# A two-layer block on one Trainium2 core: a new order in the even mixer, from the last input block to the output projection

## The reference, cut to what matters

```
def even_mixer(hn, w_in, w_conv, g_v, w_s, b_s, w_out):
    z = hn @ w_in
    b_gate, c_gate, x_in, u, v = split(z)                 # five blocks of 512 columns
    y_a = b_gate * causal_conv3(c_gate * x_in, w_conv)    # "conv half"
    u = gelu(u); v = rmsnorm_per_head(gelu(v), g_v)
    mixed = einsum('hts,nshd->nthd', tril(w_s), v) + b_s  # per head, chunks of 128 positions
    y_b = u * mixed                                       # "spatial half"
    return concatenate([y_a, y_b]) @ w_out
```

## Time and profile before

| | us |
|---|---|
| median of 3 runs | 1367.24 (1366.95 to 1367.79) |
| the profiled execution: span from its first to its last instruction | 1366.5 |
| TensorE busy | 1263.6 (92%) |
| VectorE busy | 752.9 (55%) |
| ScalarE busy | 489.6 (36%) |
| output projection of the even mixer, first product to the transposes behind it | 95.26 to 118.63 |

### The profile page before, as it was taken

How to read it: one execution, slowest core, us unless ns; L and a number is a source line. 1 busy time by engine, 2 the same in 40 slices (tenths; PEclk the granted TensorE clock), 3 DMA queues, 4 the chain that set the end, 5 groups by cost and what they waited for, 6 DMA issues and landing times.

```text
span 1366.5 us, 16254 instructions
## 1 busy us (share of the span) xinstructions
PE 1263.6 (92%) x6228; PEld 879.6 (64%) x6228; DVE 752.9 (55%) x1442; ACT 489.6 (36%) x835; POOL 27.0 (2%) x60
## 2 busy tenths in 40 slices
PE   5978999999898899999987997779999999999995
PEld 4967888876676777888866985644444444445442
DVE  4765877786657667777866998532122212222222
ACT  4424444444446444444445753411111111111111
POOL 0000000000000000000001200000000000000000
PEclk9989999999998699999998999899999999999998
DMA  8447767652431247777533311879999999999993
GB/s 274 144 156 297 255 253 252 246 185 99 163 133 62 93 179 255 252 252 253 192 126 124 124 63 62 320 315 411 410 430 426 428 431 426 431 428 430 427 427 152
DMA packets 115470, 354.66 MB, mean 260 GB/s; under 512 B 7147, under 2 KB 63140, under 8 KB 100035
## 3 DMA queue, kind: packets, MB, share of 16 engines
q1 hardware_dynamic: 109058, 328.48, 61.8%
q0 software_dynamic: 6336, 25.17, 4.7%
HBM read 352.58 MB, written 1.05 MB: 259 GB/s over the span
## 4 chain that ended last, share of the span: by engine, by line
PE 83%; DVE 9%; ACT 3%; DMA 3%; issue 1%; SPq 0%; DVEq 0%; ACTq 0%
PE ps L2593 16%; PE ps L406 14%; PE ps L408 14%; PE ps L407 14%; PE ps L2624 8%; PE ps L2582 4%; PE ps L2090 3%; DMA second_expert<-in_moe_w_up 2%; PE ps L2638 1%; DVE w_lo L380 1%; PE ps L988 1%; PE ps L2639 1%; PE ps L1766 1%; PE ps L859 1%; PE ps L1555 1%
## 5 line engine op out<-in xcount | busy, mean ns | idle before, releaser
L380 DVE TENSOR_TENSOR w_lo<-dense_weights,w_hi 128x1024 fp32r<-128x1024 f32 (+1 forms) x228 | 273.1, 1211 | 122.1 <-ACT w_hi L375 121.6
L375 ACT CAST w_hi<-dense_weights 128x1024 fp32r<-128x1024 f32 (+1 forms) x228 | 234.5, 1042 | 259.8 <-PE ps L408 236.3
L406 PE MATMUL ps<-w_hi,xT_lo 128*128 128x512 f32 (+1 forms) x624 | 251.0, 402 | 22.2 <-DVE xT_lo L2241 6.0
L407 PE MATMUL ps<-w_lo,xT_hi 128*128 128x512 f32 (+1 forms) x624 | 245.1, 393 | 0.0
L408 PE MATMUL ps<-w_hi,xT_hi 128*128 128x512 f32 (+1 forms) x624 | 244.9, 392 | 0.0
L406 PEld LDWEIGHTS ps<-w_hi,xT_lo 128*128 128x128 f32 x624 | 119.6, 192 | 51.4 <-issue 13.3
L408 PEld LDWEIGHTS ps<-w_hi,xT_hi 128*128 128x128 f32 x624 | 119.7, 192 | 25.4
L407 PEld LDWEIGHTS ps<-w_lo,xT_hi 128*128 128x128 f32 x624 | 120.1, 193 | 24.3 <-issue 0.7
L2731 DVE TENSOR_TENSOR hnT<-ps,g_bc 128x512 f32<-128x512 f32 x32 | 22.1, 692 | 157.2 <-PE ps L2624 157.2
L2740 DVE SCALAR_TENSOR_TENSOR cmask<-g_v,ps 128x256 f32<-128x256 f32 x32 | 13.5, 421 | 168.5 <-ACT g_v L2682 168.5
L2682 ACT ACTIVATE g_v<-ps 128x256 f32<-128x256 f32 x32 | 12.3, 385 | 208.2 <-PE ps L2593 208.2
(11 more groups left out here) (408 smaller groups left out, 1817.8 us busy)
## 6 DMA issues: line engine op xcount, KB each, us to landing
ada_w<-in_ada_w POOLq DMA_DIRECT2D x12, 2048.0 KB, 11.9
dense_weights<-in_w_gate SPq DMA_DIRECT2D x22, 1024.0 KB, 7.0
dense_weights<-in_w_up SPq DMA_DIRECT2D x22, 1024.0 KB, 9.3
dense_weights<-in_w_down SPq DMA_DIRECT2D x22, 1024.0 KB, 5.0
dense_weights<-in_moe_w_gate SPq DMA_DIRECT2D x11, 2048.0 KB, 18.9
dense_weights<-in_moe_w_up SPq DMA_DIRECT2D x11, 2048.0 KB, 23.4
second_expert<-in_moe_w_gate SPq DMA_DIRECT2D x11, 2048.0 KB, 17.8
second_expert<-in_moe_w_up SPq DMA_DIRECT2D x11, 2048.0 KB, 22.3
```

The source lines that it names most:

```text
L375: act.copy(split_view(w_hi, name, i, j), piece(name, i, j)).then_inc(hi_ready, 1)
L380: dve.tensor_tensor(split_view(w_lo, name, i, j), piece(name, i, j), split_view(w_hi, name, i, j).bitcast(F32), ALU.subtract).then_inc(pie ...
L406: pe.matmul(out, left[1], right[0], start=start, stop=False)
L407: pe.matmul(out, left[0], right[1], start=False, stop=False)
```

## The change

TensorE: the mixing now stands behind piece 0 of the last input block, and the turning behind piece 2. The output projection starts with the spatial half: it reads it from tiles of its own, `spatial_hi` and `spatial_lo` (in the space of `hnT`), for pieces 0 and 1, and waits for the conv half only ahead of piece 2. The rows of `w_out` are loaded in the matching order, as two copies per block. VectorE: the last input piece is split ahead of z; the bias additions and `gm_s` stand ahead of the taps; the first tap of each chunk is made by ScalarE.

```
-ITEMS = [("ev_in", 5, 1, 0), ("ev_out", 2, 1, 0), ...
+ITEMS = [("ev_in", 5, 1, 0), ("ev_out", 2, 2, 0), ...
# tokens_by_columns(..., first=None)
+                        parts = first if first is not None and j < 2 else (xT_hi, xT_lo)
+                        x = [v[:, 2 * j + kk, t * P:(t + 1) * P] for v in parts]
# weight_stream
-            columns("ev_out", a["ev_w_out"][0], [0, 512])
+            for i in range(2):
+                dst = cols8(part_a("ev_out", i))
+                load_a("ev_out", i, [dst[:, 0:4], dst[:, 4:8]], [w[:, first:first + 4, i * 512:(i + 1) * 512] for first in (4, 0)])
# EvenStage.pe
+                        if i == 2 and f == 0:
+                            self.mixing(pe)
+                        if i == 2 and f == 2:
+                            self.turning(pe)
+                pe.wait_ge(self.mix_split, 1)
+                for i in range(2):
+                    tokens_by_columns(pe, "ev_out", i, (6 - 2 * i, 7 - 2 * i),
+                                      rest=(lambda: pe.wait_ge(self.mix_split, 2)) if i == 0 else None, first=(spatial_hi, spatial_lo))
# EvenStage.act
+                split_upto(act, split_hi, "ev_out", 0, 0, ahead=0)
+                act.wait_ge(self.vn, 2)
+                for c in range(4):
+                    last = act.activation(ev_y[:, c], ev_z[:, c, 0:S], ACT.Copy, scale=col("ev_w_conv", c))
+                last.then_inc(self.u_tanh, 1)
                 split_upto(act, split_hi, "ev_out", 0, 2, ahead=0)
+                act.wait_ge(self.y_turned, 1)
+                act.copy(spatial_hi[:], ps[:, 4:6, :]...).then_inc(self.mix_hi, 1)
                 act.wait_ge(self.mixT_ready, 1)
-                act.copy(xT_hi[:, 0:4, :], mixT[:, 0:4, :]).then_inc(self.mix_hi, 1)
-                act.wait_ge(self.y_turned, 1)
-                act.copy(xT_hi[:, 4:8, :], ps[:, 4:6, :]...).then_inc(self.mix_hi, 1)
+                act.copy(xT_hi[:, 4:8, :], mixT[:, 0:4, :]).then_inc(self.mix_hi, 1)
# EvenStage.dve, the new order behind gm_u
+                split_upto(dve, split_lo, "ev_in", 4, 3, ahead=0)
                 dve.wait_ge(self.x_copied, 1)
+                dve.tensor_tensor(ev_z[:, :, 2:], ...).then_inc(self.vn, 1)
                 dve.wait_ge(self.mixed, 1)
...
+                split_upto(dve, split_lo, "ev_out", 0, 0, ahead=0)
+                dve.wait_ge(self.vn, 2)
+                dve.wait_ge(self.u_tanh, 2)
+                for j in (1, 2):
...
                 dve.wait_ge(self.mix_hi, 1)
+                dve.tensor_tensor(spatial_lo[:], ps[:, 4:6, :]..., spatial_hi..., ALU.subtract).then_inc(self.mix_split, 1)
+                split_upto(dve, split_lo, "ev_out", 0, 1, ahead=0)
+                wait_used(dve, "ev_in", 4, 3)
+                dve.tensor_tensor(mixT[:, 0:4, :], ps[:, 0:2, :]..., ev_y[:], ALU.mult).then_inc(self.mixT_ready, 1)
+                split_upto(dve, split_lo, "ev_out", 0, 2, ahead=0)
                 dve.wait_ge(self.mix_hi, 2)
+                dve.tensor_tensor(xT_lo[:, 4:8], mixT[:, 0:4], xT_hi[:, 4:8]..., ALU.subtract).then_inc(self.mix_split, 1)
```

More of the change, by code:

```diff
@@ L55 @@
 SLOTS = 2
-ITEMS = [("ev_in", 5, 1, 0), ("ev_out", 2, 1, 0), ("ffn0", FF_BLOCKS, 2, 1), ("ple0", 2, 1, 1), ("od_in", 5, 1, 0),
+ITEMS = [("ev_in", 5, 1, 0), ("ev_out", 2, 2, 0), ("ffn0", FF_BLOCKS, 2, 1), ("ple0", 2, 1, 1), ("od_in", 5, 1, 0),
          ("od_up", 2, 0, 1), ("od_out", 2, 1, 0), ("ffn1", FF_BLOCKS, 2, 1), ("ple1", 2, 1, 1), ("conv_in", 4, 2, 0),
@@ L158, in build @@
             hnT = st("hnT", [P, KC, S])
+        with scope() as st:
+            spatial_hi = st("spatial_hi", [P, 4, S], F32R)
+            spatial_lo = st("spatial_lo", [P, 4, S], F32R)
         with scope() as st:
@@ L408, in three_passes, with tokens_by_columns @@
             return pe.matmul(out, left[0], right[0], start=False, stop=stop)
-        def tokens_by_columns(pe, name, i, banks, n=512, rest=None, chunks=None):
+        def tokens_by_columns(pe, name, i, banks, n=512, rest=None, chunks=None, first=None):
             for j in range(4):
@@ L561, in weight_stream @@
             columns("ev_in", a["ev_w_in"][0], [2048, 1536, 512, 1024, 0])
-            columns("ev_out", a["ev_w_out"][0], [0, 512])
+            w = a["ev_w_out"][0].rearrange("(k p) n -> p k n", p=P)
+            for i in range(2):
+                dst = cols8(part_a("ev_out", i))
+                load_a("ev_out", i, [dst[:, 0:4], dst[:, 4:8]], [w[:, first:first + 4, i * 512:(i + 1) * 512] for first in (4, 0)])
             ffn(0)
@@ L1175, in __init__ @@
                 self.u_tanh_in = sem("ev_u_tanh_in")
-                self.u_tanh = sem("ev_u_tanh")
-                self.vn = sem("ev_vn")
+                self.u_tanh = sem("ev_u_tanh_and_first_taps")
+                self.vn = sem("ev_vn_and_z")
                 self.mixed = sem("ev_mixed")
@@ L1194, in pe, with mixing @@
                         columns_by_tokens(pe, at, halves(pe, "ev_in", 2 + i, f)).then_inc(pieces_used, 1)
+                        if i == 2 and f == 0:
[6 more added lines that the diff above has]
+                                      rest=(lambda: pe.wait_ge(self.mix_split, 2)) if i == 0 else None, first=(spatial_hi, spatial_lo))
+            def mixing(self, pe):
                 pe.wait_ge(self.vn, 1)
@@ L1202, in pe, with turning @@
                 last.then_inc(self.mixed, 1)
+            def turning(self, pe):
                 pe.wait_ge(self.y_b, 1)
@@ L1209, in pe @@
                 last.then_inc(self.y_turned, 1)
-                pe.wait_ge(self.mix_split, 2)
-                for i in range(2):
-                    tokens_by_columns(pe, "ev_out", i, (6 - 2 * i, 7 - 2 * i))
             def act(self, act):
@@ L1229, in act @@
                 act.activation(gm_s[:], gm_s[:], ACT.Tanh, scale=0.7978845608028654).then_inc(self.u_tanh, 1)
+                split_upto(act, split_hi, "ev_out", 0, 0, ahead=0)
[3 more added lines that the diff above has]
+                last.then_inc(self.u_tanh, 1)
                 split_upto(act, split_hi, "ev_out", 0, 2, ahead=0)
+                act.wait_ge(self.y_turned, 1)
+                act.copy(spatial_hi[:], ps[:, 4:6, :].rearrange("p b (c s) -> p (b c) s", c=2)).then_inc(self.mix_hi, 1)
                 act.wait_ge(self.mixT_ready, 1)
-                act.copy(xT_hi[:, 0:4, :], mixT[:, 0:4, :]).then_inc(self.mix_hi, 1)
-                act.wait_ge(self.y_turned, 1)
-                act.copy(xT_hi[:, 4:8, :], ps[:, 4:6, :].rearrange("p b (c s) -> p (b c) s", c=2)).then_inc(self.mix_hi, 1)
+                act.copy(xT_hi[:, 4:8, :], mixT[:, 0:4, :]).then_inc(self.mix_hi, 1)
                 split_upto(act, split_hi, "ev_out", 1, 3)
@@ L1270, in dve @@
                 own(dve.scalar_tensor_tensor(out=gm_u[:], in0=gm_s[:], scalar=1.0, in1=gm_u[:], op0=ALU.add, op1=ALU.mult))
+                split_upto(dve, split_lo, "ev_in", 4, 3, ahead=0)
                 dve.wait_ge(self.x_copied, 1)
[L1273 to L1286, removed]
+                dve.tensor_tensor(ev_z[:, :, 2:], ps[:, 4:6, :].rearrange("p b (c s) -> p (b c) s", c=2), ev_x[:],
+                                  ALU.mult).then_inc(self.vn, 1)
                 dve.wait_ge(self.mixed, 1)
@@ L1294, in dve @@
                                          op1=ALU.mult).then_inc(self.y_b, 1)
-                dve.wait_ge(self.mix_hi, 1)
-                dve.tensor_tensor(xT_lo[:, 0:4], mixT[:, 0:4], xT_hi[:, 0:4].bitcast(F32), ALU.subtract).then_inc(self.mix_split, 1)
+                split_upto(dve, split_lo, "ev_out", 0, 0, ahead=0)
+                dve.wait_ge(self.vn, 2)
+                dve.wait_ge(self.u_tanh, 2)
+                for j in (1, 2):
+                    for c in range(4):
+                        own(dve.scalar_tensor_tensor(out=ev_y[:, c], in0=ev_z[:, c, j:j + S], scalar=col("ev_w_conv", 4 * j + c),
+                                                     in1=ev_y[:, c], op0=ALU.mult, op1=ALU.add))
+                dve.wait_ge(self.mix_hi, 1)
+                dve.tensor_tensor(spatial_lo[:], ps[:, 4:6, :].rearrange("p b (c s) -> p (b c) s", c=2),
+                                  spatial_hi[:].bitcast(F32), ALU.subtract).then_inc(self.mix_split, 1)
+                split_upto(dve, split_lo, "ev_out", 0, 1, ahead=0)
+                wait_used(dve, "ev_in", 4, 3)
+                dve.tensor_tensor(mixT[:, 0:4, :], ps[:, 0:2, :].rearrange("p b (c s) -> p (b c) s", c=2), ev_y[:],
+                                  ALU.mult).then_inc(self.mixT_ready, 1)
+                split_upto(dve, split_lo, "ev_out", 0, 2, ahead=0)
                 dve.wait_ge(self.mix_hi, 2)
-                dve.tensor_tensor(xT_lo[:, 4:8], ps[:, 4:6, :].rearrange("p b (c s) -> p (b c) s", c=2),
-                                  xT_hi[:, 4:8].bitcast(F32), ALU.subtract).then_inc(self.mix_split, 1)
+                dve.tensor_tensor(xT_lo[:, 4:8], mixT[:, 0:4], xT_hi[:, 4:8].bitcast(F32), ALU.subtract).then_inc(self.mix_split, 1)
                 for i in range(2):
```

1 line of the change is left out of this document (removed).

## The result

The changed kernel took 1349.68 us (median of 4 executions, 1345.20 to 1352.94) against 1367.51 of before (4 executions), a ratio of 0.9868 (0.9847 to 0.9889). Two repetitions on two other chips gave 1352.74 and 1353.36, ratios 0.9893 (0.9876 to 0.9910) and 0.9898 (0.9883 to 0.9914). Over all 13 executions of the changed kernel the median is 1352.9; over all 65 of the kernel before it is 1367.7, so that the gain over everything on record is 14.8 us. The profiled execution has a span of 1351.1 us and a time of 1352.94; in every execution whose span is listed the time is 1.7 to 1.9 above the span.

The account below looks back on a forecast made before the run. It took TensorE, with its waits on VectorE and the half clock behind them, as the bound. 12.6 us gained less 0.2 for stage changes gave 12.4, so span 1354.1 and time 1354.8 us, range 1352.5 to 1358.5.

Parts of the forecast that it names:

- The new order on TensorE: Even mixer: mixing at 71.0, turning at 80.25, piece 3 to 84.25, output projection ending at 106.0 instead of 118.63.
- The operands' times: Even mixer: VectorE and ScalarE deliver each operand in time; smallest slack 0.5 us, before the output projection's first product.
- Waits removed: Even mixer: TensorE's three waits on VectorE, 3.4, 2.8 and 2.4 us, go away, 8.6 us in all.
- Low clock removed: Even mixer: half-clock time saved in piece 3 (1.7 us), turning (0.6) and output projection (1.6).
- All later stages shift as one: After the output projection: everything hangs on the sums written to h, so the remaining distance stays 1247.9 us.
- Rival C: Later stages: the same gaps meet the clock differently, giving back 2 to 5 us or adding up to 8; 18%.
- A: Even mixer: the clock falls at the turning, cutting the gain to 8.6 to 9.1 us, time 1358.3; 7%.
- B: Even mixer: VectorE becomes the bound, TensorE waits up to 1.5 us before the output projection, 1355.5 to 1356.8; 10%.
- D: From the mixing on: its 64-column products put the clock down and it stays down, 26 us more, 1381; 3%.
- E: Even mixer: mixing is late, so turning finds y_b late; 3 to 6 us of gain remain, 1361 to 1364; 2%.
- The two copies: Output weights: loading each block as two copies instead of one was taken to cost zero.
- The step from span to time: Whole kernel: the median of the runs was taken as 0.7 us above the profiled span, turning 1354.1 into 1354.8.

Follow-up runs that it names:

- e2: Changed kernel with the first tap back on VectorE instead of ScalarE; median 1355.22 us against 1352.74 for the changed kernel.
- e9: Kernel before, with 4, 3 and 2 unread products put in front of TensorE's three waits; median 1362.52 us against 1366.80, ratio 0.9965.
- e5: Kernel before, run again unaltered for a second trace; span 1364.8 us, where the first trace had 1366.5.
- e10: Changed kernel with one unread 512-column product ahead of each attention head's scores from the fourth head on; median 1349.17 us, ratio 0.9872 to the kernel before.
- e4: Changed kernel with the turning behind piece 3 of the last input block instead of ahead of it; median 1357.04 us.
- e6: Kernel before, with 7, 5 and 4 unread products put in front of TensorE's three waits; median 1365.75 us against 1367.83, ratio 0.9974.
- e12: Changed kernel run a third time, unaltered; median 1353.36 us, single executions 1352.3 to 1355.9.

## Why the prediction was wrong, point by point

The step that failed is "all later stages hang on the sums written to h, so they shift as one", with the part ahead of the change taken as fixed beside it, and with a range that did not allow for either. From the forecast of 1354.8 to the profiled execution's 1352.94 the terms are: 0.9 less ahead of the stretch, 0.4 less in it, 1.7 less behind it, and 1.1 more between span and time. From there to the median of 1349.68 another 3.3 are missing; they come from two executions of which no trace exists. So the mechanism of the change was right and its size nearly so, and what moved the result out of the range lies outside the changed stretch.

- *The new order on TensorE*: right to a tenth. From `gm_u` to the projection's end 35.2 us were worked out (106.0 - 70.8), and 35.05, 35.06 and 35.06 measured. Mixing stands 0.2 us behind `gm_u`, turning needs 1.03, no window is below full clock.
- *The operands' times*: right. The low half was wanted 0.5 us after it was ready, and 0.24 was left; the first taps took 1.71 of the 1.6 to 2.4 allowed, and e2 shows what they save (1.5 us).
- *Waits removed*, 8.6 us: right in kind, 0.6 short; e9 to after gives 9.2. The 0.2 us set against the gain for three more changes of stage did not show as a loss.
- *Low clock removed*, 3.9 us: read from one trace, where it was 3.5 (44.3 in e9 to 47.8). In that trace the two errors nearly cancel, which is luck: 12.8 us measured for 12.4. The other trace of the same kernel pays 5.1 for the same waits, so there the change is worth 14.4. The term is not one number, and the sum had no room for that.
- *All later stages shift as one*: right for the work, wrong for the time; this is the step that failed. The distance from the projection's end to the span's end was foretold as 1247.9; it is 1246.1, 1245.7 and 1248.0 after and 1247.9 and 1244.9 before. In the profiled pair 1.6 of the 1.7 us are the fall of the clock in the first feed-forward stage that the trace of before had and that of after had not. Over all traces the sections that vary are the first feed-forward (192.4 or 194.0), the second (205.7 or 207.3), the attention (177.1 to 180.2) and the last part, from the last sum written to h to the end (485.2 to 487.6). Rival C named this and bounded it by 2 to 5 us more and up to 8 less; giving it 9% on the good side, I cut the range at 1352.5.
- *The measured median*: 1349.68 is 2.8 below the range because two of its four executions took 1345.2 and 1347.7, with a mean granted clock of 0.974 and 0.973 where the two others have 0.969. Both repetitions have medians inside the range, as has the median over all 13 executions (1352.9). As an estimate, 0.005 and 0.004 more of clock over 1345 us are 6.7 and 5.4 us of TensorE's time, and these two were 7.1 and 4.6 shorter than the mean of the two others, so that a different clock would be enough to explain them. The kernel before has such executions too (1359.3 and 1359.4 among its 44 listed beside e5 and e9, clock 0.969 for 0.963), only more rarely. Whether two low ones in the first four were chance or belong to the chip of that measurement isn't shown. e10 shows one place that can give as much, 7.6 us in the attention loop. That the low executions were short there isn't shown, as none of them was traced; this stays open.
- *Rivals A, B, D, E*: not seen. By the Trainium skill's "TensorE: Matmul & The Clock Gate", Part 4, transposes don't count as busy in the way that products do; eight of them inside the stream of products did not bring the clock down in the three traces of the changed kernel (1.03 us for eight). e4, where the same eight stand ahead of a wait of 2.4 us, had a fall.
- *The two copies*: right, they cost nothing. The Trainium skill's "SBUF — State Buffer", section on the DMA setup-cost knee, gives about 2 us for each transfer; for two copies issued one behind the other against one of the same bytes no run shows such a second charge (8.87 to 9.11 us against 8.87 and 9.09). The 12.1 worked out from it had a slip besides: 12.4 less 0.2 is 12.2.
- The step from span to time was careless: the time is 1.8 above the span of the same execution, not 0.7. The profiled execution of before took some 1368.3 by that (an estimate, its time isn't on record), so the sum against its own time gives 1355.9, further from what was measured and not nearer.

## What to carry to other kernels

Put what a chain of small steps produces inside the last long run of products, and begin the next product with the operand that is ready first: here that took 9.2 us of waits away. Price a wait of TensorE at its length plus what half clock behind it costs, and take that second part from several executions: the same three waits cost 3.5 us in one and 5.1 in another. Where a gain is worked out from one profile, make the range as wide as the clock's falls in the unchanged stages: here 3.1 us between the five traces of the table, and more between single executions.

## What the runs showed of the hardware

- TensorE can be busy without a pause and still run at 1.2 GHz: 12.00 of 12 us at 0.50 in the attention loop. One 512-column product per head that nobody reads brought the loop to 2.4 GHz and made its section 7.6 us shorter than in the shortest other trace, though it adds work (e10).
- A float32 product of 512 columns that isn't split by hand shows as two instructions of 0.43 us (e6).
- The records give a clock of 1.00 at the start, but the first products of the input projection run at half rate for a while, until about 19.9 in the first trace of before, 19.3 in e5 and 18.3 in the changed kernel: 0.42 us from start to start, where 0.23 is the full rate. With the first product at 17.9, 17.8 and 17.7, `gm_u` is then at 70.8, 70.4 and 69.9, so this is nearly all of the 0.9 us ahead of the stretch. (In e12, where `gm_u` is at 71.1, the clock fell between 40 and 50 us.) Why the half rate lasts longer in one execution than in another isn't shown. TensorE's timeline of e5:

```profile
18.34 0.63 PE L407 MATMUL ps<-w_lo,xT_hi 128*128 128x512 f32 x1
18.76 0.63 PE L408 MATMUL ps<-w_hi,xT_hi 128*128 128x512 f32 x1
...
19.48 0.39 PE L407 MATMUL ps<-w_lo,xT_hi 128*128 128x512 f32 x1
```
